# A macaron, convolution and latent-attention decoder layer on one core: the opening stage rebuilt, with products of ones ahead of the rows, sums of squares taken from rows, and the first two column tiles among the transposes

## The chip, the cores and the metric

One core of a Trainium2 chip runs the whole layer. The metric is the device time in microseconds. Three runs of the kernel before gave 1726.42, 1723.62 and 1724.4 us; their median is 1724.4 us.

## What is computed

One layer on 576 tokens (512 of a prompt, 64 new ones of eight sequences), 1024 channels, float32:

```
x = x + 1/2 * SwiGLU_FFN1(rmsnorm(x))
P = rmsnorm(x) @ w_in -> [GLU input | q_a | c_kv | k_pe | gate_a | gate_b]
A = conv branch (GLU, causal depthwise conv 31, LayerNorm, swish, projection)
B = latent attention with rotary keys, causal softmax, paged cache for the new tokens
x = x + w_out( sigmoid(gate_a) * A + sigmoid(gate_b) * B )
x = x + 1/2 * SwiGLU_FFN2(rmsnorm(x))
rmsnorm(x) = x * rsqrt(mean(x*x) + 1e-6) * g
swiglu_ffn(x) = (silu(h @ w_g) * (h @ w_u)) @ w_down,  h = rmsnorm(x), inner width 2816
```

The change touches only the start: the first rmsnorm and the first four of the 44 weight chunks of the first up-projection.

## The kernel before

**Layout.** The residual stream is kept transposed in SBUF: `xT` holds eight column tiles of 128 channels by 576 tokens (`KD` = 8, `T` = 576, `HALF` = 288). Every large product is made in three passes of fp32r: `x_hi` and `w_hi` are the rounded values, `x_lo` and `w_lo` what is left of them, and `product` (line 366) adds `w_hi*x_hi`, `w_hi*x_lo` and `w_lo*x_hi`, each over two halves of 288 tokens. So one column tile k of one weight chunk is 6 matmuls, and one chunk (8 tiles, 128 output channels) is 48. The row scale of rmsnorm (`rstd`) is applied to the outputs, not to x; so the products can start before it is known, but the first hidden tile can't be read out.

**Weights.** Chunk n (0, 1: gate and value columns of hidden tile 0; 2, 3: of tile 1; and so on) goes through a ring of 4 raw buffers and 2 hi buffers. SyncE's queue loads it in two DMAs (`load_chunk`, line 337); ScalarE copies it to `w_hibuf` (`split_hi`, 350), which from the third chunk on waits until chunk n-2 has been used up; GpSimd subtracts in four pieces (`split_lo`, 357), and TensorE waits for `w_lo_done` (`chunk`, 986).

**Opening.** SyncE issues the 5 DMAs of x rows (lines 462, 463) and then the 8 DMAs of chunks 0 to 3. ScalarE's queue issues 13 DMAs of gains, convolution weights and tables (661 to 670). TensorE waits for all 13 constants (`const_in`, 968), transposes the gains and the convolution weights, and then the x rows, 5 transposes for each column tile (973 to 984). VectorE copies each tile from PSUM to `xT` (1391, 1392), and one tile later makes `x_lo` (1371) and adds the squares into `sumsq` (1375, 1378). ScalarE makes square and `x_hi` of each tile (678, 679), with the hi copies of chunks 0 and 1 between tiles 0 and 2 (line 696). Only after all the transposes does TensorE begin chunk 0, tile by tile as `x_lo` comes (`x_ready`, 1004); `sums` (996) adds the squares over the partitions with a matrix of ones ahead of chunk 1; VectorE inverts (`inverse`, 1380), ScalarE takes the root (`rstd_root`, 681).

**Order that is written out by hand.** Each engine runs its own list in order. ScalarE's is `second_pair_hi` (708: hi of chunk 2, the root, hi of chunk 3), then `hidden(0)` (685: Silu, then `a_hi`), and only then the loop's `up_hi`, whose first item is the hi copy of chunk 4. VectorE's `hidden` (1402) scales the two products by `rstd` (1400), multiplies (1412) and makes `a_lo` (1414). TensorE needs the first PSUM unit read out, and the lo pieces of chunk 4, before it can start chunk 4.

Of the kernel before, what the change touches and what calls it, by code (L numbers as in the profile page):

```python
# [14 lines left out]
F32 = mybir.dt.float32  # L15
# [15 lines left out]
NT = PT_TILES + 1  # L31
DFF = 2816
# [21 lines left out]
KN, SQ = HH * DN, HH * DS_  # L54
KQ = KN + SQ
# [25 lines left out]
def layer(nc, x_prompt, x_sample, cache_ckv, cache_kpe, state_conv, page_table, w, const, out):  # L81

    ctx = ExitStack()
    with ctx:
# [50 lines left out]
        x_nat = place("x_nat", [P, NT, D], F32, A0 + 2 * XB)  # L135
        gain_rows = place("gain_rows", [NG, P], F32, A0 + 2 * XB + 4 * NT * D)
        conv_rows = place("conv_rows", [W, C], F32, A0 + 2 * XB + 4 * NT * D + 4 * P)
# [102 lines left out]
        stat = ps[:, 5:8, HALF:HALF + T // 3]  # L240


        const_in = sem("const_in")
# [191 lines left out]
        def _(sp):  # L435
# [25 lines left out]
            for i in range(PT_TILES):  # L461
                sp.dma_start(x_nat[:, i, :], x_prompt[0, i * P:(i + 1) * P, :]).then_inc(x_in, 16)
            sp.dma_start(x_nat[0:TS, PT_TILES, :], x_sample.rearrange("s t d -> (s t) d")).then_inc(x_in, 16)
            load_up(wv, n_ffn1_up, 0, 0, wait=False)
            load_up(wv, n_ffn1_up, 1, 1, wait=False)
# [103 lines left out]
        def _(pool):  # L569
            pool.memset(ones[:, :], 1.0).then_inc(ones_done, 1)  # L570

# [4 lines left out]
            with pool.Fori(0, FT // 2) as i:  # L576
                lo4(i * 4 + n_ffn1_up, n_ffn1_up, KD * P)
# [81 lines left out]
        def _(act):  # L659

            for name, row, k in (("norm_ffn1", G_FFN1, KD), ("norm_mix", G_MIX, KD), ("norm_ffn2", G_FFN2, KD),
                                 ("conv_b", G_CB, CT), ("conv_ln_g", G_LG, CT), ("conv_ln_b", G_LB, CT),
                                 ("q_a_norm", G_QA, QL // P)):
                act.dma_start(gain_rows[row:row + k, :], w[name][0].rearrange("(k p) -> k p", p=P)).then_inc(const_in, 16)
            act.dma_start(conv_rows[:, :], w["conv_w"][0]).then_inc(const_in, 16)
            act.dma_start(ident[:, :], const["ident"]).then_inc(const_in, 16)
            act.dma_start(causal[:, :], const["causal"]).then_inc(const_in, 16)
            act.dma_start(rope[:, :, :, :], const["rope"]).then_inc(const_in, 16)
            act.dma_start(kvg[:, :], w["kv_a_norm"][0:1, :].broadcast_to([P, KL])).then_inc(const_in, 16)
            act.dma_start(gqk[:, :], w["q_head_norm"][0:1, :].broadcast_to([P, DH])).then_inc(const_in, 16)  # L670

            def x_parts(v, t, c, gain, x_hi=x_hi):

                act.wait_ge(x_done, t + (KD * v + 1))
                if v or not isinstance(t, int) or t >= 2:
                    act.wait_ge(acc_done, t + (KD * v - 1))
# [4 lines left out]
            def rstd_root(v):  # L681
                act.wait_ge(inv_done, v + 1)
# [92 lines left out]
            act.wait_ge(acc_done, 2 * KD)  # L775
# [190 lines left out]
        def _(pe):  # L966

            pe.wait_ge(const_in, 13 * 16)
            pe.transpose(ps[:, 7, 0:NG], gain_rows[:, :], ident[0:NG, 0:NG])
            for c in range(CT):  # L970
                tr = pe.transpose(ps[:, 7, NG + c * W:NG + (c + 1) * W], conv_rows[:, c * P:(c + 1) * P], ident[0:W, 0:W])
            tr.then_inc(tr_done, 1)
            pe.wait_ge(x_in, 80)
            for t in range(KD):
                if t == 3:
                    pe.wait_ge(unit_read, 4)
                if t >= 4:
                    pe.wait_ge(x_done, t - 3)
# [967 lines left out]
```

## Time and profile before

| | before |
|---|---|
| median of 3 runs | 1724.4 us |
| the profiled execution's own time | 1725.19 us |
| its span | 1723.4 us |
| TensorE busy | 1633.0 us, 95% |
| VectorE, ScalarE, GpSimd busy | 744.2, 529.6, 603.8 us |
| HBM read | 117.79 MB |

A profile is one execution. The span is counted from its first instruction, and windows are microseconds from there. A matmul's duration holds the time that it spends in the pipe, so how fast matmuls go is read from start to start. The column PEclk is the granted TensorE clock as a share of 2.4 GHz; the clock's first record lies at about 36 us, and the profile prints 1.00 for everything ahead of it.

### The profile page before, as it was taken

What the parts mean: (1) busy time and instruction counts of PE and PEld (TensorE: products, weight loads), DVE (VectorE), ACT (ScalarE), POOL (GpSimd) and SP (SyncE); (2) the same over time, 40 slices, a digit from 0 to 9 for tenths busy, and PEclk for the clock granted to TensorE, in tenths of its full rate; (3) what the DMA queues carried; (4) which work ended last, traced back from release to release, by engine and by line L of the source; (5) the groups of instructions that cost most, each with busy time, mean ns of one, the idle gap of its engine ahead of it and who ended that gap; (6) DMA issues with size and microseconds to landing.
All of it is one profiled execution on the core that took longest, in us unless ns stands there. A gap on an engine that the chain in (4) does not pass through costs nothing.

```text
span 1723.4 us, 31031 instructions
## 1 busy us (share of the span) xinstructions
PE 1633.0 (95%) x11549; PEld 1545.2 (90%) x11549; DVE 744.2 (43%) x1148; ACT 529.6 (31%) x920; POOL 603.8 (35%) x693
## 2 busy tenths in 40 slices
PE   5999999999899999787999999999999999999998
PEld 4999999999899988365988888887999999999997
DVE  5322222212169866754566666664643222221001
ACT  3222222222221232242444444552333222222110
POOL 2455455444345545100000000001565455554441
PEclk9999999999999999897899999999999999999999
DMA  4222223222233322001212221212222222223221
GB/s 121 80 85 83 75 85 90 87 83 84 62 85 89 108 70 63 0 1 50 50 45 55 56 55 53 56 29 62 74 86 86 74 84 85 82 76 102 85 84 55
DMA packets 230066, 122.13 MB, mean 71 GB/s; under 512 B 28223, under 2 KB 226983, under 8 KB 229972
## 3 DMA queue, kind: packets, MB, share of 16 engines
q1 hardware_dynamic: 229150, 120.56, 24.3%
q8 instruction: 47, 0.77, 0.2%
q10 hardware_dynamic: 830, 0.48, 0.1%
q14 instruction: 39, 0.32, 0.1%
HBM read 117.79 MB, written 3.58 MB: 70 GB/s over the span
## 4 chain that ended last, share of the span: by engine, by line
PE 81%; DVE 8%; issue 4%; ACT 3%; POOL 2%; SPq 1%; DMA 1%; ACTq 0%; DVEq 0%; POOLq 0%
PE ps L376 61%; PE ps L1283 9%; PE ps L1226 3%; POOL w_lobuf L362 2%; PE ps L1133 1%; PE ps L1106 1%; PE ps L1212 1%; ACT prob L822 1%; DVE y L1455 1%; DVE page_ss L1848 1%; PE ps L1113 1%; PE ps L1252 1%; DMA gqk<-in_q_head_norm 1%; DVE s_buf L1740 1%; SPq L521 1%
## 5 line engine op out<-in xcount | busy, mean ns | idle before, releaser
L362 POOL TENSOR_TENSOR w_lobuf<-w_rawbuf,w_hibuf 128x256 fp32r<-128x256 f32 (+1 forms) x664 | 579.2, 903 | 651.8 <-ACT w_hibuf L355 651.8
L376 PE MATMUL ps<-x_hi,w_hibuf 128*128 128x288 f32 x1888 | 409.3, 298 | 6.8 <-POOL w_lobuf L362 3.1
L376 PE MATMUL ps<-x_lo,w_hibuf 128*128 128x288 f32 x1888 | 407.8, 298 | 0.0
L376 PE MATMUL ps<-x_hi,w_lobuf 128*128 128x288 f32 x1888 | 407.6, 297 | 0.0
L355 ACT ACTIVATE w_hibuf<-w_rawbuf 128x1024 fp32r<-128x1024 f32 (+1 forms) x166 | 185.2, 1115 | 667.7 <-PE ps L376 667.7
L376 PEld LDWEIGHTS ps<-x_hi,w_hibuf 128*128 128x128 f32 x1888 | 305.6, 189 | 9.0 <-issue 4.5
L376 PEld LDWEIGHTS ps<-x_lo,w_hibuf 128*128 128x128 f32 x1888 | 305.8, 189 | 0.4
L376 PEld LDWEIGHTS ps<-x_hi,w_lobuf 128*128 128x128 f32 x1888 | 305.6, 189 | 0.4
L376 PE MATMUL ps<-a_hi,w_lobuf 128*128 128x288 f32 x704 | 151.1, 296 | 0.0
L376 PE MATMUL ps<-a_hi,w_hibuf 128*128 128x288 f32 x704 | 151.0, 296 | 0.0
L376 PE MATMUL ps<-a_lo,w_hibuf 128*128 128x288 f32 x704 | 151.0, 296 | 0.0
L1400 DVE TENSOR_TENSOR tb<-ps,rstd 128x576 f32<-128x576 f32 x48 | 36.3, 757 | 248.2 <-PE ps L376 248.2
L1283 PE MATMUL ps<-kq_hi,cT_hi 128*128 128x288 f32 x512 | 125.4, 326 | 7.2 <-DVE cT_lo L1718 7.2
L1848 DVE TENSOR_REDUCE page_ss<-sq 128x8 f32<-128x512 f32 x128 | 85.0, 680 | 95.1 <-ACT sq L897 94.7
L1429 DVE SCALAR_TENSOR_TENSOR xT<-ps,xT 128x576 f32<-128x576 f32 x24 | 18.2, 758 | 247.7 <-PE ps L376 247.7
L644 POOL TENSOR_TENSOR ta<-kpe_nat 128x512 f32<-128x512 f32 x8 | 8.6, 1070 | 315.7 <-DMA kpe_nat<-in_cache_kpe 315.7
L376 PEld LDWEIGHTS ps<-a_hi,w_lobuf 128*128 128x128 f32 x704 | 113.7, 188 | 0.0
L376 PEld LDWEIGHTS ps<-a_hi,w_hibuf 128*128 128x128 f32 x704 | 113.7, 188 | 0.0
L376 PEld LDWEIGHTS ps<-a_lo,w_hibuf 128*128 128x128 f32 x704 | 113.7, 188 | 0.0
L1283 PE MATMUL ps<-kq_hi,cT_lo 128*128 128x288 f32 x512 | 110.4, 297 | 0.0
L1283 PE MATMUL ps<-kq_lo,cT_hi 128*128 128x288 f32 x512 | 110.3, 297 | 0.0
L1455 DVE SCALAR_TENSOR_TENSOR y<-ext,cols,y 128x512 f32<-128x512 f32 x120 | 104.5, 871 | 2.5
(266 smaller groups left out, 1992.0 us busy)
## 6 DMA issues: line engine op xcount, KB each, us to landing
w_rawbuf<-in_ffn_w_gu SPq DMA_DIRECT2D x176, 256.0 KB, 3.1
c_nat<-in_cache_ckv SPq DMA_DIRECT2D x128, 128.0 KB, 2.1
w_rawbuf<-in_w_in SPq DMA_DIRECT2D x58, 256.0 KB, 3.1
w_rawbuf<-in_ffn_w_down SPq DMA_DIRECT2D x32, 384.0 KB, 3.7
w_rawbuf<-in_ffn_w_down SPq DMA_DIRECT2D x32, 320.0 KB, 3.0
w_rawbuf<-in_w_out SPq DMA_DIRECT2D x16, 256.0 KB, 3.0
x_nat<-in_x_prompt SPq DMA_DIRECT2D x4, 512.0 KB, 4.9
w_rawbuf<-in_w_conv_out SPq DMA_DIRECT2D x8, 256.0 KB, 3.3
```

The lines of the kernel that those rows point to most:

```text
L355: act.activation(w_hibuf[:, r % HIS, 0:size], w_rawbuf[:, r, 0:size], ACT.Copy).then_inc(w_hi_done, 1)
L362: ins = pool.tensor_tensor(w_lobuf[:, r, part], w_rawbuf[:, r, part], w_hibuf[:, r % HIS, part].bitcast(F32), ALU.subtract)
L376: mm = pe.matmul(ps[0:width, 2 * s + h, 0:HALF], a, b[:, k, h * HALF:(h + 1) * HALF], start=first and i == 0 and j == 0, stop=last and i = ...
L521: page = sp.value_load(pages[0:1, ds(s * NP + t, 1)], min_val=0, max_val=cache_ckv.shape[1] - 1)
L822: act.activation(prob[:, qi, 0:(qi + 1) * P], ps[:, 2 + qi, 0:(qi + 1) * P], ACT.Exp, bias=small[:, 1, qi:qi + 1], scale=SCALE, accum_out= ...
L1106: mm = pe.matmul(ps[0:n, 2 * s + b, 0:QL], qaT[k][:, i * P:i * P + n], w_uq[:, k, b * QL:(b + 1) * QL], start=k == 0, stop=k == QL // P - 1)
L1226: mm = pe.matmul(ps[0:HQ, 7, 0:KL], s_buf[:, b, t, :], c_nat[:, b, t, :], start=t == 0, stop=False)
L1283: mm = pe.matmul(ps[:, page_banks(t) + half, 0:KQ], a, m[:, half, cols], start=k == 0 and j == 0, stop=k == 1 and j == 2)
L1400: return dve.tensor_tensor(halves(dst), unit(s)[0:rows], halves(rstd[0:rows, :]), ALU.mult)
L1429: dve.scalar_tensor_tensor(x2, unit(s), scale, x2, op0=ALU.mult, op1=ALU.add).then_inc(x_done, 1)
L1455: dve.scalar_tensor_tensor(dst, src, cw, dst, op0=ALU.mult, op1=ALU.add).then_inc(conv_p_step, 1)
L1848: dve.tensor_reduce(page_ss[:, t, :], sq[:, u, 0:H * DN].rearrange("p (h d) -> p h d", d=DN), AX, ALU.add).then_inc(page_red, 1)
```

## The change

It makes these edits.

1. The x rows are cut into six groups (128, 128, 32, 128, 128, 32 tokens) that don't cross the middle of the 576, and loaded by 7 DMAs. SyncE issues chunk 0 after them, waits for all x rows, issues chunk 1, waits for chunk 0, and issues chunks 2 and 3.
2. ScalarE's queue issues the identity and the first gain ahead of the other gains and the convolution weights; causal mask, rotary table, `kvg` and `gqk` are issued later, by `late_constants`, after the root in `second_pair_hi`. TensorE waits for two constants at the start instead of 13.
3. TensorE runs 30 products of a 128x128 matrix of ones with itself first.
4. Transposes of a tile use two PSUM units in turn. VectorE copies a tile with one instruction and makes its `x_lo` from PSUM right after ScalarE's `x_hi` of the same tile. TensorE puts the transposes of tile k+2 behind the product of chunk 0 with tile k, and then chunk 1 with tile k-4.
5. The squares are summed by ScalarE from the six row groups (with an accumulator); VectorE and ScalarE make the inverse root of a 128x6 tile; VectorE spreads it over six diagonal tiles; after chunk 2, TensorE transposes the other constants and multiplies the diagonals by ones (8 products), and VectorE copies the result to `rstd`.
6. The lo parts of chunks 0 and 1 are signalled piece by piece.

```diff
+X_GROUPS = ((0, 128), (128, 128), (256, 32), (288, 128), (416, 128), (544, 32))
+WARM = 30
@@ sync
+            for g, (t0, n) in enumerate(X_GROUPS):
+                prompt = max(0, min(n, TP - t0))
+                if prompt:
+                    sp.dma_start(x_nat[0:prompt, g, :], x_prompt[0, t0:t0 + prompt, :]).then_inc(x_in, 16)
+                if prompt < n:
+                    sp.dma_start(x_nat[prompt:n, g, :], new[t0 + prompt - TP:t0 + n - TP, :]).then_inc(x_in, 16)
+            load_chunk(sp, 0, 0, wv, 0, KD, 0, P, wait=False)
+            sp.wait_ge(x_in, 7 * 16)
+            load_chunk(sp, 1, 1, wv, 0, KD, DFF, P, wait=False)
+            sp.wait_ge(w_in_sem[0], 32)
+            load_chunk(sp, 2, 2, wv, 0, KD, P, P, wait=False)
+            load_chunk(sp, 3, 3, wv, 0, KD, P + DFF, P, wait=False)
@@ gpsimd
+            pool.memset(x_ss[:, :], 1.0).then_inc(ones_done, 1)
+            for n in range(2):
+                pool.wait_ge(w_hi_done, n + 1)
+                for c in range(4):
+                    part = slice(c * KD * P // 4, (c + 1) * KD * P // 4)
+                    pool.tensor_tensor(w_lobuf[:, n, part], w_rawbuf[:, n, part], w_hibuf[:, n, part].bitcast(F32), ALU.subtract)\
+                        .then_inc(w_piece, 1)
+                pool.wait_ge(w_piece, 4 * n + 4)
+                pool.sem_inc(w_lo_done, 1)
@@ scalar
+            act.dma_start(ident[:, :], const["ident"]).then_inc(rows_in, 16)
...
+            def row_squares(g):
+                n = X_GROUPS[g][1]
+                act.activation(x_sq[0:n, :], x_nat[0:n, g, :], ACT.Square, accum_out=x_ss[0:n, g:g + 1]).then_inc(x_squared, 1)
+                act.wait_ge(x_squared, g + 1)
+            act.wait_ge(x_in, 7 * 16)
+            act.wait_ge(ones_done, 2)
             act.wait_ge(unit_read, 4)
             for t in range(KD):
-                x_parts(0, t, t, G_FFN1)
                 if t < 2:
                     split_hi(act, t, t, KD * P, free=False)
+                act.wait_ge(x_done, t + 1)
+                act.activation(x_hi[:, t, :], xT[:, t, :], ACT.Copy, scale=cols[:, G_FFN1 + t:G_FFN1 + t + 1]).then_inc(xh_done, 1)
+                if t % 2 and t < KD - 1:
+                    row_squares(t // 2)
+            row_squares(3)
@@ second_pair_hi
                 split_hi(act, n0 + 2, (n0 + 2) % RAWS, KD * P)
-                rstd_root(v)
+                if v:
+                    rstd_root(v)
+                else:
+                    row_squares(4)
+                    row_squares(5)
                 split_hi(act, n0 + 3, (n0 + 3) % RAWS, KD * P)
+                if not v:
+                    act.wait_ge(x_inv, 1)
+                    act.activation(x_ss[:, :], x_ss[:, :], ACT.Sqrt).then_inc(x_root, 1)
+                    late_constants()
@@ tensor
+            pe.wait_ge(ones_done, 1)
+            for _ in range(WARM):
+                pe.matmul(ps[:, 0, 0:P], ones[:, :], ones[:, :], start=True, stop=True)
+            pe.wait_ge(rows_in, 2 * 16)
+            pe.transpose(ps[:, 3, 0:KD], gain_rows[0:KD, :], ident[0:KD, 0:KD]).then_inc(tr_done, 1)
+            pe.wait_ge(x_in, 7 * 16)
+            def x_transposes(t):
+                if t >= 2:
+                    pe.wait_ge(xl_done, t - 1)
+                for g, (t0, n) in enumerate(X_GROUPS):
+                    tr = pe.transpose(ps[:, 4 + 2 * (t % 2) + t0 // HALF, t0 % HALF:t0 % HALF + n],
+                                      x_nat[0:n, g, t * P:(t + 1) * P], ident[0:n, 0:n])
                 tr.then_inc(tr_done, 1)
+            def first_pair():
+                LAG = 4
+                x_transposes(0)
+                x_transposes(1)
+                pe.wait_ge(unit_read, 4)
+                for k in range(KD):
+                    first_chunk(0, k)
+                    if k + 2 < KD:
+                        x_transposes(k + 2)
+                    if k >= LAG:
+                        first_chunk(1, k - LAG)
+                for k in range(KD - LAG, KD):
+                    first_chunk(1, k)
+            def first_rstd():
+                pe.wait_ge(const_in, 7 * 16)
...
+                pe.wait_ge(x_spread, 1)
...
+                            mm = pe.matmul(stat0[:, b, a - b * third:z - b * third], ones[0:n, :], x_diag[0:n, g, a - t0:z - t0],
+                                           start=True, stop=True)
+                mm.then_inc(x_rstd, 1)
@@ ffn, the first one
+                    first_pair()
+                    chunk(2, 2, q_up + 2, (q_up + 2) % 4, range(KD), x_hi, x_lo)
+                    first_rstd()
+                    chunk(3, 3, q_up + 3, (q_up + 3) % 4, range(KD), x_hi, x_lo)
+                    up_pair(n_up, q_up, 2, 0, **x)
+                    pe.wait_ge(tables_in, 4 * 16)
@@ vector
             for t in range(KD):
+                xs = ps[:, 4 + 2 * (t % 2):6 + 2 * (t % 2), 0:HALF]
                 dve.wait_ge(tr_done, t + 2)
+                dve.tensor_copy(halves(xT[:, t, :]), xs).then_inc(x_done, 1)
+                dve.wait_ge(xh_done, t + 1)
+                dve.scalar_tensor_tensor(halves(x_lo[:, t, :]), xs, cols[:, G_FFN1 + t:G_FFN1 + t + 1],
+                                         halves(x_hi[:, t, :]).bitcast(F32), op0=ALU.mult, op1=ALU.subtract).then_inc(xl_done, 1)
+            dve.wait_ge(x_squared, NX)
...
+            for g in range(NX):
+                n = X_GROUPS[g][1]
+                ins = dve.tensor_scalar(x_diag[0:n, g, 0:n], ident[0:n, 0:n], x_ss[0:n, g:g + 1], None, ALU.mult)
+            ins.then_inc(x_spread, 1)
+            dve.wait_ge(x_rstd, 1)
+            dve.tensor_copy(rstd[:, :].rearrange("p (b n) -> p b n", b=3), stat0)
+            dve.tensor_copy(cols[:, KD:NCOL], ps[:, 3, HALF + KD:HALF + NCOL]).then_inc(rstd_done, 1)
```

## Rows read from the trace of the kernel before

**Rows 1.** Busy time of each engine by stretch: window, length, busy (instructions), PEclk, DMA share, GB/s.
```profile
0.00:40.00 40.00, 20.91 (x92) 16.84 (x93) 20.05 (x34) 13.77 (x19) 8.06 (x13) 1.00 0.43 123
84.00:200.00 116.00, 116.00 (x873) 116.00 (x872) 29.00 (x36) 30.42 (x36) 60.19 (x72) 1.00 0.27 81
```

**Rows 2.** Chain that ended last, 0 to 80 us: start, us, what.
```profile
6.02 10.11 DMA gqk<-in_q_head_norm
...
41.34 38.67 PE ps L376 x290
```

**Rows 3.** Timeline 0 to 30 us: start, us, engine, line, operation, idle before.
```profile
0.72 0.20 POOL L570 MEMSET ones<- 128x128 f32 x1 [0.29 <-POOLq L1936]
...
4.96 0.54 ACTq L668 DMA_DIRECT2D rope<-in_rope  x1
...
18.03 1.01 PEld L982 LDWEIGHTS ps<-ident,x_nat 64*128 64x128 f32 x5 [0.33 <-issue]
...
19.37 1.01 PEld L982 LDWEIGHTS ps<-ident,x_nat 64*128 64x128 f32 x5 [0.33 <-issue]
...
19.41 1.28 ACT L678 ACT_TABLE_LOAD   x1 [19.41 <-DVE xT L1392]
```

**Rows 4.** Arrival of the x rows and weights: us from issue to landing, 0 to 45 us.
```profile
L463 SPq DMA_DIRECT2D x_nat<-in_x_sample x1: 644/644/644, 2.6 to 2.6; - x1
DMA to landing us min/median/max: 3.6/5.4/7.6
```

**Rows 5.** Busy time by stretch, 8 to 12 us (last column: GB/s).
```profile
8.00:12.00 4.00, 0.00 (x0) 0.00 (x0) 0.00 (x0) 0.00 (x0) 0.00 (x0) 1.00 1.13 257
```

**Rows 6.** VectorE's, ScalarE's instructions by line, duration ns min/median/max.
```profile
L1371 DVE SCALAR_TENSOR_TENSOR x_lo<-xT,cols,x_hi x8: 802/819/1233, 22.1 to 38.4; 128x576 fp32r<-128x576 f32 x8
L1400 DVE TENSOR_TENSOR ta<-ps,rstd x22: 758/758/758, 46.9 to 310.2; 128x576 f32<-128x576 f32 x22
L679 ACT ACTIVATE x_hi<-xT,cols x8: 757/760/762, 21.3 to 37.6; 128x576 fp32r<-128x576 f32 x8
L355 ACT ACTIVATE w_hibuf<-w_rawbuf x5: 1039/1057/1062, 22.0 to 54.2; 128x1024 fp32r<-128x1024 f32 x5
```

**Rows 7.** Timeline 30 to 70 us, chunks 0 and 1 and the first hidden tile.
```profile
30.46 0.82 PE L376 MATMUL ps<-x_hi,w_hibuf 128*128 128x288 f32 x2 [1.88 <-DVE xT L1392]
...
35.39 0.68 PE L376 MATMUL ps<-x_lo,w_hibuf 128*128 128x288 f32 x2
...
35.87 0.68 PE L376 MATMUL ps<-x_hi,w_lobuf 128*128 128x288 f32 x2
...
40.20 1.14 PE L1001 MATMUL ps<-sumsq,ones 128*128 128x192 f32 x6
...
41.60 2.82 POOL L362 TENSOR_TENSOR w_lobuf<-w_rawbuf,w_hibuf 128x256 fp32r<-128x256 f32 x4 [10.87 <-ACT w_hibuf L355]
...
48.91 1.28 ACT L688 ACT_TABLE_LOAD   x1
...
51.79 0.69 ACT L690 ACTIVATE a_hi<-tb 128x576 fp32r<-128x576 f32 x1 [0.90 <-DVE tb L1412]
...
54.18 1.06 ACT L355 ACTIVATE w_hibuf<-w_rawbuf 128x1024 fp32r<-128x1024 f32 x1 [1.70 <-PE ps L376]
```

**Rows 8.** Timeline near 60 us, TensorE at the end of chunk 3.
```profile
60.24 0.32 PEld L376 LDWEIGHTS ps<-x_hi,w_hibuf 128*128 128x128 f32 x2
```

**Rows 9.** Timeline 606 to 632 us, TensorE: transposes, a wait, products.
```profile
615.09 3.49 PE L1082 MATMUL ps<-ident,latT 128*128 128x128 f32 x24
621.43 1.46 PE L1082 MATMUL ps<-ident,latT 128*64 128x128 f32 x6 [2.85 <-DVE lat L1536]
622.82 0.85 PE L376 MATMUL ps<-x_hi,w_hibuf 128*128 128x288 f32 x2
...
627.18 0.43 PE L376 MATMUL ps<-x_hi,w_hibuf 128*128 128x288 f32 x2
```

**Rows 10.** Busy time by stretch: prompt attention, 778 to 781 us.
```profile
778.00:781.00 3.00, 2.51 (x22) 2.20 (x21) 2.65 (x7) 1.40 (x4) 0.00 (x0) 1.00 0.00 0
```

More of the change, by code:

```diff
@@ L31 @@
 NT = PT_TILES + 1
+X_GROUPS = ((0, 128), (128, 128), (256, 32), (288, 128), (416, 128), (544, 32))
+NX = len(X_GROUPS)
 DFF = 2816
@@ L458, in load_merge @@
                 sp.dma_start(dst[:, CT:KD, :], src[:, :, (t + 1) * P:(t + 2) * P]).then_inc(w_in_sem[n % RAWS], 16)
[L461 to L465, printed above, removed]
+            new = x_sample.rearrange("s t d -> (s t) d")
+            for g, (t0, n) in enumerate(X_GROUPS):
[10 more added lines that the diff above has]
+            load_chunk(sp, 3, 3, wv, 0, KD, P + DFF, P, wait=False)
             with sp.Fori(1, FT // 2) as i:
@@ L574, in lo4 @@
                     split_lo(pool, n + g, (n0 + g) % RAWS, size)
-            with pool.Fori(0, FT // 2) as i:
+            for n in range(2):
[6 more added lines that the diff above has]
+                pool.sem_inc(w_lo_done, 1)
+            for n in range(2, 4):
+                split_lo(pool, n, n, KD * P)
+            with pool.Fori(1, FT // 2) as i:
                 lo4(i * 4 + n_ffn1_up, n_ffn1_up, KD * P)
@@ L774, in _ @@
             act.wait_ge(filled, 2)
-            act.wait_ge(acc_done, 2 * KD)
+            act.wait_ge(acc_done, KD)
             for i in range(NT):
@@ L966, in _ @@
         def _(pe):
[L968 to L978, printed above, removed]
-                for i in range(NT):
-                    n = P if i < PT_TILES else TS
-                    c = (i % PT_TILES) * P
-                    tr = pe.transpose(ps[:, 2 * (t % 4) + i // PT_TILES, c:c + n],
-                                      x_nat[0:n, i, t * P:(t + 1) * P], ident[0:n, 0:n])
-                tr.then_inc(tr_done, 1)
+            pe.wait_ge(ones_done, 1)
@@ new lines, in first_chunk @@
+            def first_chunk(n, k):
+                pe.wait_ge(xl_done, k + 1)
+                pe.wait_ge(w_piece, 4 * n + k // 2 + 1)
+                mm = product(pe, n, n, range(k, k + 1), x_hi, x_lo, w0=k, first=k == 0, last=k == KD - 1)
+                if k == KD - 1:
+                    mm.then_inc(w_used, 1)
+            def first_pair():
[11 more added lines that the diff above has]
+                    first_chunk(1, k)
@@ new lines, in first_rstd @@
+            def first_rstd():
+                pe.wait_ge(const_in, 7 * 16)
+                pe.transpose(ps[:, 3, HALF:HALF + NG], gain_rows[:, :], ident[0:NG, 0:NG])
+                for c in range(CT):
+                    pe.transpose(ps[:, 3, HALF + NG + c * W:HALF + NG + (c + 1) * W], conv_rows[:, c * P:(c + 1) * P], ident[0:W, 0:W])
+                pe.wait_ge(x_spread, 1)
+                pe.wait_ge(ones_done, 1)
+                third = T // 3
+                for g, (t0, n) in enumerate(X_GROUPS):
+                    for b in range(3):
+                        a, z = max(t0, b * third), min(t0 + n, (b + 1) * third)
+                        if a < z:
+                            mm = pe.matmul(stat0[:, b, a - b * third:z - b * third], ones[0:n, :], x_diag[0:n, g, a - t0:z - t0],
+                                           start=True, stop=True)
+                mm.then_inc(x_rstd, 1)
@@ L1363, in _ @@
         def _(dve):
+            dve.memset(tb[:, :], 0.0).then_inc(al_done, 1)
             dve.wait_ge(tr_done, 1)
-            dve.tensor_copy(cols[:, :], ps[:, 7, 0:NCOL]).then_inc(unit_read, 4)
-            dve.memset(tb[:, :], 0.0).then_inc(al_done, 1)
+            dve.tensor_copy(cols[:, G_FFN1:G_FFN1 + KD], ps[:, 3, 0:KD]).then_inc(unit_read, 4)
             def x_low(v, t, c, gain, hi, lo):
```

68 lines of the change are left out of this document (38 added, 30 removed).

## The prediction

> **What bounds the kernel now.** I read the busy times by stretch first. From 84 to 200 us TensorE is busy in every microsecond and issues 873 matmuls in 116 us, 0.133 us each; in the first 40 us it is busy for 20.9 [rows 1]. So only the opening has slack to win, and what is won there moves all that follows, since TensorE is the chain from 41.34 us on [rows 2]. The end point of my sum is the first matmul of chunk 4: chunk 1 begins at about 41.0, and three chunks of 48 matmuls at 0.133 us (6.4 us) put chunk 4 at 60.24 [rows 2, 8].
>
> The chain shows what the opening is made of: TensorE waits until 16.1 us for the last constant, `gqk` [rows 2]; eight tiles of transposes at 1.34 us each follow (from 18.03 to 19.37) [rows 3]; products start at 30.46 and chunk 0 ends at 40.2, held by VectorE, which makes a copy, `x_lo` and a sum of squares of each tile [rows 7].
>
> **TensorE's clock.** The clock column has no record here, so I read the level from the pace. Pairs of products go every 0.48 us (35.39 to 35.87), 0.24 us for one of 288 columns, which is 1.2 GHz, and stay at this until about 36.2, 5.8 us after the products began [rows 7]; later one goes every 0.133 us, 2.4 GHz [rows 1]. The nine microseconds of transposes from 17 us on did not raise it. At 615 us 24 transposes and a wait of 2.85 us are followed by products at the low level (durations 0.85), and it is high again at 627.2, 4.4 us after they began [rows 9]. A mixed stretch in which TensorE is busy for 2.51 of 3 us keeps the high level [rows 10].
>
> **The change, part by part** (times from the start of the span).
>
> *Constants and rows.* The wait for `gqk` goes. What is late next is the x rows: the last landed 7.6 us after its issue at 2.6, so at 10.2 [rows 4]; with 4 small tables out of the way I take 9.8 (9.3 to 10.2). Chunk 0's 512 KB come behind them on the same queue; at 257 GB/s [rows 5] that is 2 us, so 12 us (11.5 to 13.2).
>
> *Products of ones.* They start at 0.97, when the ones are set (0.72+0.20) [rows 3]. The profile shows a float32 product as two matmuls: three products of 192 columns are 6 in 1.14 us, 0.163 apart [rows 7], so 0.108 for 128 columns at the high level, 0.133 if the weight load sets the pace, and 0.213 at the low one. Of 60, 27 pass in the 5.8 us that the clock took in rows 7; 33 more take 3.6 to 4.4: the end is at 10.4 to 11.2. Never raised, it is 60 x 0.213 = 12.8, so 13.8. I take 11.0. It hides the wait for the rows, and is 1.2 us longer.
>
> *To the first `x_lo`.* Gain transpose, copy to `cols`: unit_read at 11.6. ScalarE now waits for chunk 0 (12.0) ahead of its first instruction, then table load 1.28 [rows 3], hi copy 1.04, `x_hi` 0.76 [rows 6]: 15.2. `x_lo` has only one SBUF input now besides PSUM; the nearest row is the scaling from PSUM, 0.758 in all 22 [rows 6], not the 0.80 to 1.23 of L1371 beside GpSimd. With 0.1 for semaphores: 16.1. GpSimd's first piece (0.7) is in time.
>
> On the table load the row shows 1.28 us. The Trainium skill (ScalarE: Activation LUTs, What ACT_TABLE_LOAD costs) adds about 1.38 us of drain to each switch. At 48.91 the load ends at 50.19, and multiply and `a_hi` end by 52.48 [rows 7], which leaves no room for a drain; with the page's figure my sum would be some 2.8 us later (two loads on the path), without it it stands.
>
> *Tiles 1 to 7.* They are now serial between VectorE and ScalarE: copy 0.76, `x_hi` 0.76, `x_lo` 0.76, 0.1 of semaphores, 2.4 us a tile (2.3 to 2.6). ScalarE's hi copy of chunk 1 (1.06) and the squares of the row groups (about 1.3 by L355's 1.06 plus an accumulator read) lie in the time in which VectorE works on. If TensorE keeps up, `x_lo` of tile 7 is there at 16.1+7x2.4 = 32.9, and five parts of 0.8 us (tile 7 of chunk 0, tiles 4 to 7 of chunk 1) end the pair at 36.9; with TensorE's own excess at tiles 4 and 5 I say **37.5**.
>
> *Does it keep up?* Between 11 and 16.1 TensorE has only tiles 0 and 1 to transpose and waits some 2.5 us. That is the picture of rows 9, after which the clock was low. At the low level a product part takes 6x0.24 = 1.44, a tile's transposes 1.6 (1.34 [rows 3] and a second cut at 32 rows), so 3.05 us for tiles 0 to 3 and 4.5 where chunk 1 joins: more than VectorE's 2.4. Tile 4's turn begins at 16.1+4x3.05 = 28.3 and ends at 32.8; high from there, tile 5's takes 2.6, and eight parts of 0.8 are left: **41.8, I take 42**. High from 28.3 on gives 40; only at 37.3, 44; still low in the last parts, 45.
>
> The Trainium skill (TensorE: Matmul & The Clock Gate, What's actually happening) says that "the default state is throttled, and activity releases the throttle". By that rule alone the products of ones release it and the opening is fast, my first rival; rows 9 speak for the low level instead.
>
> *Chunk 2.* Its hi copy waits for the end of chunk 0, 4.0 us ahead of the pair's end; 1.06 for hi, 2.82 for lo [rows 7] and 0.2: a wait of 0.1 to 1.2. I take 0.5. Then 6.4.
>
> *Root on TensorE.* Today `sums` costs 1.1 ahead of chunk 1. Now 5 small transposes and 16 matmul instructions of 32 to 128 columns come after chunk 2: bounds 1.0 (as today's sums) and 3.1 (0.163 each and 0.5); I take 2.4, nearer to the weight loads' pace. ScalarE's root and VectorE's six diagonals are hidden under chunk 2 (6.4 us). The four late DMAs are at most 0.54 each on ScalarE's queue [rows 3], 2.2 us, under chunk 2 as well; uncovered they would cost that.
>
> *Chunk 3, then chunk 4.* Here a new wait appears. The hi copy of chunk 4 stands on ScalarE behind `hidden(0)`, which now can't start until the sums behind chunk 2. Today `a_hi` ends at 52.48, 1.70 ahead of the release of that copy at 54.18 [rows 7]. After: copy of `rstd` 0.76, rest of `cols` 0.3, scaling 0.76, table load to the end of `a_hi` 3.57 (48.91 to 52.48), hi 1.06, lo 2.82 to 3.9, semaphores 0.4: 9.7 to 10.8 us, against 6.4 of chunk 3. TensorE waits 3.3 to 4.4 us; I take 3.4. Chunks 5 and on have their slack back.
>
> *Sum* for the pair's end at 42: 0.5+6.4+2.4+6.4+3.4 = 19.1, so chunk 4 at 61.1 against 60.24: +0.9. The wait of 3.4 us can let the clock fall once more, which rows 9 price at some 2 us (4.4 us of products at half pace); at 3 in 10 that is +0.6. **+1.5 us.** The profiled execution's own time is 1725.19 (span 1723.4), so 1726.7 by it; it lay 0.8 above the median of the three runs, and I state the forecast against the median: 1724.4+1.5, rounded to **1726.0 us**. Its own range is 1724 to 1728. About 0.2%, 3.45 us, is what a measurement of this kernel tells from no change.
>
> **Rivals.**
> 1. *The clock stays high.* Pair's end 37.5, chunk 4 at 56.6: -3.6 us, 1720.8; with sums of 1.0 us, 1719.4. For it: the mixed stretch of rows 10. Against: that stretch has no wait of 2.5 us. Chance 0.20, over half of it beyond 0.2%.
> 2. *The low clock lasts until products stand alone* (slower). TensorE's turn at tiles 0 to 5 is the place, 3.05 and 4.5 us against 2.4. It decides if the level is still low at about 35 us: pair's end 44 to 45, chunk 4 at 63.1 to 64.1, +3 to +4, and +2 when the wait at chunk 4 drops the clock: some 1729.5. For it: transposes among the products, which alone never raised it. Against: TensorE has no gaps then. Chance 0.26, 0.22 beyond 0.2%.
> 3. *No wait at chunk 4*, because VectorE and ScalarE are through sooner than their order says: 3.4 and 0.6 less, 1722; with a high clock 1717. Against: the order is fixed. Chance 0.12, 0.08 beyond.
> 4. *The products of ones don't raise the clock.* They end at 13.8, all parts are low: pair's end 46 or later, 1730 or more. Against: products raised it in both rows. Chance 0.08.
>
> The forecast keeps 0.34, nearly all within 0.2%. So faster 0.12+0.08 = 0.20, slower 0.22+0.06 to 0.08 and a little of the forecast = 0.32, same 0.48. The range: 1719.5 leaves out the low end of rivals 1 and 3, 1730.5 that of rivals 2 and 4, some 0.2 together.
>
> **What would show it.** Right: ones ending near 11; first product near 16; pace 0.24 from there to about 33; the pair's end near 42; a wait of TensorE for `w_lobuf` of 3 to 4 us ahead of chunk 4. Wrong: pace 0.133 all through, sums under 1 us, or no wait at chunk 4. If VectorE's step is over 2.6 us a tile, my term for the serial chain is the fault.

## The result, and the profile after

| | before | after |
|---|---|---|
| median of 6 runs each | 1724.6 us | 1731.2 us (1730.5 to 1733.4) |
| the profiled execution's own time | 1725.19 us | 1731.6 us |
| its span | 1723.4 us | 1729.8 us |
| first product | 30.46 us | 19.29 us |
| end of chunks 0 and 1 | 47.5 us | 47.5 us |
| chunk 2, 3, 4 begin | 47.58, 53.98, 60.38 us | 47.82, 57.31, 65.59 us |

The ratio is 1.0039, 95% interval 1.0026 to 1.0052: 6.6 us slower, just above the forecast range (1719.5 to 1730.5) and 5.2 us above the forecast of 1726.0. The first matmul of chunk 4 starts at 60.38 us before (the row of [rows 8], 60.24, is the last weight load of chunk 3) and at 65.59 after, so the opening alone explains 5.2 us. Two runs of the experiments below, of 1818.1 and 2022.2 us at mean granted clocks of 0.84 and 0.74, fell into a slow state of the chip and are in no median.

Busy times by stretch of the kernel after, in the columns of [rows 1]:

```profile
2.00:10.00 8.00, 8.00 (x58) 7.88 (x57) 0.00 (x0) 0.00 (x0) 0.00 (x0) 1.00 1.00 299
12.00:16.00 4.00, 3.18 (x12) 1.69 (x12) 0.76 (x1) 0.68 (x1) 0.00 (x0) 0.53 0.57 161
16.00:20.00 4.00, 0.71 (x3) 0.74 (x4) 1.48 (x2) 3.38 (x5) 2.25 (x4) 0.50 0.84 237
28.00:39.00 11.00, 11.00 (x43) 8.78 (x42) 5.04 (x7) 3.87 (x7) 0.00 (x0) 0.50 0.00 0
39.00:40.00 1.00, 1.00 (x6) 0.56 (x4) 0.00 (x0) 0.00 (x0) 0.00 (x0) 0.71 0.00 0
40.00:47.00 7.00, 7.00 (x52) 6.82 (x52) 1.58 (x2) 4.98 (x8) 2.06 (x3) 1.00 0.25 73
```

Here the clock column has records, the first at 5.5 us. Until then the matmul instructions of the products of ones start every 0.213 us, from then on every 0.111 us: the level rose there. It fell at 12.3 us (0.53 over 12 to 16), when TensorE had waited 1.7 us for the x rows and had just begun their transposes; the longer wait for chunk 0, from 15.2 to 19.3, came after that. It stayed at 0.50, which is 1.2 GHz, through the steps of the tiles, and rose only at 39.6 (0.71 over 39 to 40). Between 28 and 39 TensorE is busy in every microsecond and still issues only 43 matmuls.

The chain of waits after, 4 to 66 us (start, us, what), shows what the engines waited for:

```profile
4.75 10.48 DMA w_rawbuf<-in_ffn_w_gu
...
15.32 1.28 ACT L368
16.61 1.06 ACT w_hibuf L368
17.67 0.67 ACT x_hi L741
18.34 0.02 issue
18.37 0.83 DVE x_lo L1497
19.20 0.09 issue
19.29 1.78 PE ps L389 x6
21.07 1.53 PE ps L1036 x6
22.59 1.74 PE ps L389 x6
24.33 1.53 PE ps L1036 x6
```

Chunk 0 lands at 15.2 us, and from there to 19.3 everything waits for the row of table load, hi copy, `x_hi` and `x_lo`. Then TensorE alone is the chain: a product part and the transposes of a tile, 3.27 us together. The timeline after (as in [rows 3, 7]) has the waits of the other engines:

```profile
11.92 3.26 PE L1036 MATMUL ps<-ident,x_nat 128*128 128x128 f32 x12 [1.70 <-DMA x_nat<-in_x_sample]
...
22.63 0.76 DVE L1495 COPY xT<-ps 128x576 f32<-128x576 f32 x1 [1.12 <-PE ps L1036]
...
54.97 2.42 PE L1077 MATMUL ps<-x_diag,ones 128*128 128x128 f32 x16
...
65.59 0.54 PE L389 MATMUL ps<-x_hi,w_hibuf 128*128 128x288 f32 x2 [1.62 <-POOL w_lobuf L375]
```

The copy of a tile waits for TensorE, not the other way round. The root stage goes from 54.3 to 57.31, and at chunk 4 TensorE waits for `w_lobuf`, whose hi copy stands behind the first hidden tile.

### The profile page after: what moved, and what is told of

Same layout as the page of the kernel before. It is cut to its first block, busy times and chain, and to the rows that moved or that the text cites. A ratio compares the mean times of both kernels' runs of the same rounds, so it can differ in the third digit from the quotient of the medians.

```text
span 1729.8 us, 31160 instructions
## 1 busy us (share of the span) xinstructions
PE 1649.6 (95%) x11628; PEld 1558.5 (90%) x11628; DVE 737.1 (43%) x1140; ACT 531.0 (31%) x924; POOL 601.3 (35%) x694
## 4 chain that ended last, share of the span: by engine, by line
PE 81%; DVE 7%; issue 4%; ACT 3%; POOL 2%; SPq 1%; DMA 1%; DVEq 0%; ACTq 0%; POOLq 0%
PE ps L389 61%; PE ps L1386 9%; PE ps L1329 3%; POOL w_lobuf L375 2%; PE ps L1236 1%; PE ps L1209 1%; PE ps L1315 1%; ACT prob L878 1%; DVE y L1569 1%; DVE page_ss L1962 1%; PE ps L1216 1%; DMA w_rawbuf<-in_ffn_w_gu 1%; PE ps L1355 1%; DVE s_buf L1854 1%; SPq L542 1%
## 5 line engine op out<-in xcount | busy, mean ns | idle before, releaser
L375 POOL TENSOR_TENSOR w_lobuf<-w_rawbuf,w_hibuf 128x256 fp32r<-128x256 f32 (+2 forms) x656 | 570.9, 901 | 643.9 <-ACT w_hibuf L368 643.9
```

What stands on the lines that cost most here:

```text
L375: ins = pool.tensor_tensor(w_lobuf[:, r, part], w_rawbuf[:, r, part], w_hibuf[:, r % HIS, part].bitcast(F32), ALU.subtract)
```

## The experiments

No kernel here leaves a part of the computation out; products of ones are extra work and their results are not used. Behind each expectation stand the median time and its ratio to the kernel before on the same chip (median 1724.7 to 1725.3 us), with the 95% interval. Moments inside a kernel are read from one profiled execution of it.

**The products of ones.** Left out:

```diff
-WARM = 30
+WARM = 0
```

> The changed kernel without the 30 products of ones. Clock theory: the level they raised was lost at 12.3 us, before the first product of weights at 19.3, so they buy nothing: within 1 us of the changed kernel, first product still near 19.3 and pace 0.24 us until about 39. Rival: they are worth the transposes' speed or bring the later rise forward; without them it is slower by 2 us or more.

1732.0 us, ratio 1.0034 (1.0020 to 1.0048). The first product came at 19.77 and the level rose at 44.6. The medians don't tell this version from the kernel after (1731.2, ratio 1.0039). In the profiled executions chunk 4 began 2.2 us later without the ones (67.83 against 65.59), since the level rose 5 us later, but the moment of the rise varies from run to run, as shown below. So no gain by the 30 products in front is shown: their high level is gone before the first product of weights. Held over the gap instead, with 8 more in front:

```diff
-WARM = 30
+WARM = 38
@@ first_pair, behind x_transposes(1)
+                for _ in range(20):
+                    pe.matmul(ps[:, 0, 0:P], ones[:, :], ones[:, :], start=True, stop=True)
```

> The changed kernel with 38 products of ones ahead of the rows and 20 more between the transposes of tile 1 and the first product of weights (TensorE idles there from 15.2 to 19.25). Clock theory: the level stays high, VectorE's 2.4 us a tile sets the step instead of TensorE's 3.27, and the pair ends near 41 instead of 47.5: 6 us faster than the changed kernel, about 1725. Rival (rows, weights and the serial chain are the cost, not the clock): less than 1.5 us faster, or slower by the 20 products if they run late.

1724.2 us (9 runs), ratio 1.0004 (0.9991 to 1.0016): by the ratio nearly all of the 6.6 us of the change are gone, though the first product came only 0.3 us earlier (19.03). Two of the nine runs took 1730.9, with a mean granted clock of 0.976 against 0.981 in the other seven. Busy times by stretch of this kernel, beside those above:

```profile
16.00:20.00 4.00, 3.65 (x31) 3.48 (x31) 1.48 (x2) 3.39 (x5) 2.51 (x4) 1.00 0.89 257
28.00:39.00 11.00, 10.61 (x74) 9.62 (x74) 4.88 (x7) 6.53 (x11) 1.02 (x2) 1.00 0.07 18
```

The same 11 us take 74 matmuls instead of 43, at 1.00 instead of 0.50 (from 33.15 us on they are products alone, since this kernel is further on). Chunk 2 began at 40.87 instead of 47.82. The clock over the opening is worth what the change lost. The 38 in front without the 20 in the gap were not run, so this run doesn't say which of the two groups did it.

**The table load.** A one-column Square at the start loads the table early:

```diff
+            act.activation(sq[:, 0, 0:1], ones[:, 0:1], ACT.Square)
             act.wait_ge(x_in, 7 * 16)
```

> The changed kernel with one small activation on ScalarE at the start, so that the table load lies in the wait for the rows. Chain theory: the first product comes 1.3 us earlier (18.0) and all after it, 1730.0. Rival: the step of 3.27 us is fixed by TensorE but its start moves too, so it gives the same 1.3; if it gives nothing, the start of the chain is elsewhere (arrival of chunk 0's weights at 15.3).

1730.5 us, 1.0027 (1.0016 to 1.0038). First product 1.5 us earlier (17.79), but the level rose at 42.4 instead of 39.6, and chunk 2 began at 48.0 against 47.8. While the pair runs at the low level, a start brought forward is given back if the rise comes later. That the early table made it come later is not shown: the version with ScalarE's order changed (below) has the program of the kernel after up to chunk 2, and in its profiled execution the level rose at 44.4 instead of 39.6. Over the seven profiled executions whose tiles all ran at the low level, the rise came either 18.7 to 20.3 us behind the first product, in or right behind the first twelve matmuls that follow each other without transposes (after, and two versions below), or 24.6 to 24.8 us behind it, in the last 24 (here, without the ones, and two versions below).

**The constants alone**, on the kernel before: identity first, the four tables late.

```diff
+            act.dma_start(ident[:, :], const["ident"]).then_inc(const_in, 16)
...
-            pe.wait_ge(const_in, 13 * 16)
+            pe.wait_ge(const_in, 9 * 16)
```

> The kernel before, with one part of the change alone: identity first on ScalarE's queue, the four tables issued after the root, TensorE waits for 9 constants instead of 13. Part theory: the wait for gqk until 16.1 us was the only thing ahead of the transposes, the x rows were there at 10.2; all that follows moves by 5 to 6 us, 1719 us. Rival: the weights of chunk 0 (landed by 13.2) or VectorE's steps take up the gain: less than 2 us faster.

1723.3 us, 0.9989 (0.9980 to 0.9999). Waits of this kernel, 0 to 40 us (us in total, times, longest):

```profile
PE ps L973 <- DMA conv_rows<-in_conv_w: 13.8, 1, 13.8
```

A wait until 16.1 became one until 13.8, and that is the 2 us. With the DMA of `conv_rows` moved to second place:

> e1_tables with one more move: the convolution weights' DMA right behind the identity's. In e1_tables TensorE still waited for them until 13.83 us, with the x rows there at about 10.3. If the queue's order is the reason, TensorE starts at 10.5 to 11.5 and the time falls by 2 to 3 us below e1_tables, about 1720.5. Rival: ScalarE's hi copies then wait for chunk 0's weights (13.2), and only 1 us is gained.

1722.9 us, 0.9987 (0.9977 to 0.9996); TensorE waited until 13.76, now for `gain_rows`. So the order on the queue is not what holds them. With 44 products of ones in that wait:

> e1_tables (order of the kernel before) with 44 products of ones while TensorE waits for the constants. Theory: in the old order VectorE's three operations per tile (2.1 to 3.1 us) set the pace, and TensorE at the high level only ends chunk 0 sooner by the few tenths it is behind: 0 to 1 us faster than e1_tables. Rival: the low level costs the old order too, half of the 5.7 us of products at half pace, 2 to 3 us.

1722.9 us, 0.9986 (0.9977 to 0.9996). The level was high from 6.6 to 23.7 and low again when the products began at 27.48. It is the result of the run without them.

**x rows on another queue**: the three DMAs of 32 rows on ScalarE's.

```diff
+                if row == G_FFN1:
+                    act.dma_start(x_nat[0:32, 2, :], x_prompt[0, 256:288, :]).then_inc(x_in, 16)
...
```

> The changed kernel with the three 32-row DMAs of x on ScalarE's queue instead of SyncE's. In the changed kernel the first transpose of x waits until 11.92 us, against rows complete at 10.2 before. If the small DMAs hold up the queue, the rows are complete by about 10.5 and chunk 0's weights by 14; if the DMA engines' total work is the limit, within 0.3 us of 11.9. The time itself stays within 1 us of the changed kernel either way, since the clock's rise sets the pair's end.

One run, 1733.3 us. Its timeline:

```profile
2.62 0.74 ACTq L699 DMA_DIRECT2D x_nat<-in_x_sample  x1
...
11.84 2.31 PE L1038 MATMUL ps<-ident,x_nat 128*128 128x128 f32 x12 [0.89 <-DMA x_nat<-in_x_sample]
```

The last DMA of rows was issued at 2.6 us, as in the kernel before, and the first transpose of x still waited for it until 11.84 (11.92 after); chunk 0 landed at 15.9. So the moment of issue is not what makes the rows late.

**ScalarE's order at chunk 4**: its hi copy ahead of the first hidden tile, the loop's first pass written out.

```diff
+                    split_hi(act, n0 + 4, n0 % RAWS, KD * P)
+                    hidden(f, q0, 0, a_hi)
+                    split_hi(act, n0 + 5, (n0 + 1) % RAWS, KD * P)
+                    hidden(f, q0, 1, a_hi)
```

> The changed kernel with ScalarE's list put in another order: the hi copy of chunk 4 ahead of the first hidden tile, that of chunk 5 ahead of the second. If the 1.9 us that TensorE idles before chunk 4 come only from this order, they go, and all behind moves by 1.9: about 1.6 to 1.9 us faster than the changed kernel. Rival: the lo copy or the PSUM unit (read out from 58.7 on) is just as late, and nothing changes.

1728.2 us, 1.0015 (1.0005 to 1.0025), 3.0 us less than after. The wait is gone: chunk 3 began at 59.37 and chunk 4 6.5 us later, at 65.87, where the kernel after took 8.3 us. So the order is worth 1.8 us; the rest of the 3.0 is not explained. In this profiled run, the slowest of ten, chunk 3 was itself late, since the level rose at 44.4.

**All of these together**: g1's order, the early table, `WARM` 36, and in the gap 5 products of ones, the transposes of the constants and 9 more products.

> The changed kernel with the clock kept high (36 products of ones ahead, 14 more in the gap), the table loaded at the start, the transposes of the other constants in the gap too, and the order of g1. Sum: pair's end 40.9 as in e3_fill, less 1.4 for the table; 0.6 less behind chunk 2; no wait at chunk 4: chunk 4 at about 54.7 against 60.4 before, 5.5 us faster than the kernel before, 1719.5. Rival: the fill runs late (14 products and the constants outlast the hi copy, or conv_rows lands after 14 us) and eats 1 to 2 us of it; or the clock falls after all, then 1725.

1720.4 us (1718.9 to 1722.4), 0.9972 (0.9962 to 0.9981). The clock stayed high, first product 17.72, chunk 4 at 54.8. This kernel is the base of the next two. Without its first 36 products:

> g2_best without the 36 products of ones ahead of the rows; the 14 in the gap stay. Clock theory: transposes and 14 products from 11.4 on start at the low level, don't raise it before the first product, and TensorE's step stays at 3.27 us: the pair ends at 46 to 49, 6 to 8 us slower than g2_best, near 1727. Rival: the products in the gap alone are enough, within 1 us of g2_best.

1727.0 us, 1.0006 (0.9996 to 1.0016), in two clusters: 1724 to 1726 and 1728 to 1729. The level rose at 23.0, fell at 29.8 and rose at 40.1. So the products in the gap alone are not enough, as the 30 in front alone were not. With VectorE's copy of tile t+1 ahead of `x_lo` of tile t:

> g2_best with VectorE copying tile t+1 before it makes x_lo of tile t, so that ScalarE's x_hi no longer lies in VectorE's step. With the clock high the step of 2.35 us is VectorE's serial chain; it becomes copy plus x_lo, 1.6 us, and TensorE (0.8 + 1.1, and 2.7 where chunk 1 joins) sets the pace: the pair's end moves from 39.5 to about 37, 2.3 us faster than g2_best, 1718. Rival: ScalarE's squares of the rows, or the weights of chunk 1 (17.0), hold it: under 1 us.

1731.9 us, 1.0040 (1.0026 to 1.0054): my expectation fell. Waits of this kernel, 16 to 45 us:

```profile
DVE xT L1511 <- PE ps L1045: 18.2, 6, 3.4
PEld ps L389 <- DVE x_lo L1518: 7.8, 6, 1.7
```

TensorE issues the transposes of tile t+1 behind the product of tile t-1, and VectorE now held `x_lo` of tile t back for them. The loop of both waits made the first step 3.5 us (17.93 to 21.47); at 22.8 the clock fell, and from then on a step took 4.9 us.

**What holds chunk 0's weights.** Their arrival is the term of the forecast that failed: 12.0 forecast, 15.2 measured. SyncE issues chunk 1 only when chunk 0 has landed, on the kernel after, and on the best version with 9 fewer products in the gap:

```diff
             load_chunk(sp, 0, 0, wv, 0, KD, 0, P, wait=False)
-            sp.wait_ge(x_in, 7 * 16)
-            load_chunk(sp, 1, 1, wv, 0, KD, DFF, P, wait=False)
             sp.wait_ge(w_in_sem[0], 32)
+            load_chunk(sp, 1, 1, wv, 0, KD, DFF, P, wait=False)
```

> Edit: the changed kernel, with SyncE issuing chunk 1 only when chunk 0 has landed (after the change it is issued once the x rows have landed, at 11.9 us, and chunk 0 lands at 15.2 although the DMA engines move only 20 to 40 GB/s from 12.4 to 12.9 us). Theory A (chunk 0's last pieces are held up by chunk 1 on the same queue): chunk 0 lands at 12.9 to 13.5 instead of 15.2, the table load begins there, but chunk 1 then lands 1 to 2 us later than today, about 16.5 to 17, and its hi copy stands on ScalarE ahead of the x_hi of tile 1, so the first product comes at 17.0 to 17.5 and the second no sooner than 21; the clock is low in both, and the time stays within 2 us of 1731.2. Theory B (chunk 0 is late by itself): it lands at 15.2 or later, chunk 1 at 18 or later, and the kernel is 1 to 3 us slower than the changed one.

> Edit: the best version so far (table loaded early, products of ones in the gap, chunk 4's hi copy first), with chunk 1 issued only when chunk 0 has landed, its hi copy on ScalarE moved from ahead of tile 1's x_hi to ahead of tile 2's, and the second group of nine products of ones left out. Theory A (chunk 1 holds up chunk 0's last pieces): chunk 0 lands at about 13, first product at 15.6 to 16.0 (17.7 in the best version), clock high all through, chunk 4 at about 53 (54.8), 1718 to 1719.5 us against 1720.4. Theory B (chunk 0 is late by itself): it lands at 15 as before, first product at 17.7 to 18, and without the nine products the clock falls near 20 us, so chunk 4 comes at 60 or later and the time is 1725 or more.

1730.8 us, 1.0034 (1.0023 to 1.0046), and 1725.7 us, 1.0001 (0.9993 to 1.0010). Chunk 0 landed at 15.4 and 14.9, with nothing behind it: theory A fell. In the second, the shorter filling also cost the level in eleven of twelve runs (clocks 0.974 to 0.977; the twelfth, 0.982, took 1719.4). The first one shows what does hold it. DMA of this kernel, 12.6 to 13.0 us:

```profile
DMA packets 8, 0.01 MB, mean 24 GB/s; under 512 B 1, under 2 KB 4, under 8 KB 8
## 3 DMA queue, kind: packets, MB, share of 16 engines
q10 hardware_dynamic: 4, 0.01, 5.5%
q1 hardware_dynamic: 4, 0.00, 1.5%
```

Shares of 5.5% and 1.5% of sixteen engines are one engine and a little (0.88 and 0.24). Its packets alternate: one of the constants' queue (q10), one of the weights' (q1). The packets of 2 KB on q10 are the 31 rows of `conv_rows`. Read one by one from the trace, each starts when the one before has ended, from 9.4 us to 14.0: they are all on one DMA engine, and chunk 0's share of that engine goes between them. So `conv_rows` issued late (behind chunk 2's hi copy), on the kernel after and on the best version, and `conv_rows` split on the kernel with the constants alone:

```diff
-            act.dma_start(conv_rows[:, :], w["conv_w"][0]).then_inc(const_in, 16)
+            act.dma_start(conv_rows[0:16, :], w["conv_w"][0, 0:16, :]).then_inc(const_in, 16)
+            act.dma_start(conv_rows[16:W, :], w["conv_w"][0, 16:W, :]).then_inc(const_in, 16)
```

> Edit: the changed kernel, with the DMA of the convolution weights (31 rows of 2 KB) issued on ScalarE's queue behind the hi copy of chunk 2 instead of at the start. In the trace of the run with chunk 1 issued later, these 31 packets run one after the other on a single DMA engine until about 14.0 us, and 512-byte packets of chunk 0 alternate with them after all the other engines have gone idle at 12.4. Theory C (that one DMA engine holds up chunk 0): chunk 0 lands at 12.6 to 13.3 instead of 15.2, the first product comes at 16.5 to 17.2 (19.3), the rise of the clock is up to 2.5 us earlier, and the time is 1728.5 to 1731, since the clock is still low. Theory D (the convolution weights are a bystander): chunk 0 lands at 15 or later, the time is 1730.5 to 1732.

> Edit: the best version so far with the same late DMA of the convolution weights; the transposes of the constants go back behind chunk 2, and 7 products of ones fill the wait for chunk 0 instead of 14 and the transposes. Theory C: chunk 0 lands at 12.6 to 13.3, first product at 15.6 to 16.3 (17.7), clock high all through, the pair's end 1.5 to 2 us earlier, 1.0 us more for the root stage, which has the transposes again: chunk 4 at 53.5 to 54.5 (54.8), 1718.5 to 1720.5 us. Theory D: chunk 0 lands at 15, the first product waits 2 us behind the 7 products of ones and the clock falls: 1724 us or more.

> Edit: the version of the kernel before with the identity first and the four tables late, its convolution weights loaded in two DMAs, of 16 rows and of 15 rows. Theory C (all 31 rows go to one DMA engine, and TensorE waits for that engine until 13.8 us): if 16 rows are spread over the 16 DMA engines and only the other 15 share one, the constants are there at 12.0 to 12.8, the first product comes 1.0 to 1.8 us earlier than 28.1, and the time is 1721.5 to 1722.8 against 1723.3. If both halves go to one engine, or under theory D, TensorE waits until 13.5 to 14.2 and the time stays at 1723.

Late, after: 1729.1 us, 1.0024 (1.0012 to 1.0035); chunk 0 landed at 13.3 instead of 15.2:

```profile
13.36 1.28 ACT L368 ACT_TABLE_LOAD   x1 [13.36 <-DMA w_rawbuf<-in_ffn_w_gu]
```

The first product came at 17.32, the level rose at 36.7, and chunk 4 began at 63.25, 2.3 us earlier than after. Split: 1719.7 us, 0.9973 (0.9963 to 0.9982), about 3 us less than the version without the split (0.9989) and more than either theory gave, since the packets of the second part, of 15 rows, overlap too. Timelines of the first transposes, of that version and of the split one:

```profile
13.83 0.32 PE L973 MATMUL ps<-ident,gain_rows 39*128 39x39 f32 x1 [13.83 <-DMA conv_rows<-in_conv_w]
```

```profile
10.79 0.32 PE L974 MATMUL ps<-ident,gain_rows 39*128 39x39 f32 x1 [10.79 <-DMA conv_rows<-in_conv_w]
...
25.07 0.82 PE L376 MATMUL ps<-x_hi,w_hibuf 128*128 128x288 f32 x2 [1.88 <-DVE xT L1399]
```

The constants are there 3.0 us sooner, the products begin 3.0 us sooner (28.11 to 25.07), and the 2 KB packets now overlap, all within 7.7 to 9.5 us. Theory C stands. The kernel before has this hold-up too: its 31 packets run from 8.5 to 12.9 us. The late version of the best kernel took 1723.5 us, 0.9983 (0.9973 to 0.9992), in two clusters: five runs at 1718.0 to 1719.5 (0.981 to 0.982) and seven at 1723.3 to 1725.4 (0.976 to 0.979). To see whether TensorE's short waits in a tile's step let the clock fall, I built the best version with the split, 32 products in front and 2 instead of 9 behind the constants, and a twin with one product of ones more in each of the first four steps:

```diff
                         x_transposes(k + 2)
+                    if k < LAG:
+                        pe.matmul(ps[:, 2, 0:P], ones[:, :], ones[:, :], start=True, stop=True)
```

> Edit: the version with the table early, the gap filled and chunk 4's hi copy first, its convolution weights loaded in two DMAs of 16 and 15 rows, still at the start; 32 products of ones ahead of the rows, and in the gap 5 products, the transposes of the constants and 2 more products. Expected by theory C: constants there by 11.5, chunk 0 at 12.5 to 13.3, first product at 15.6 to 16.2 (17.7), no transposes of constants behind chunk 2, chunk 4 at 52.5 to 53.5 (54.8): 1718 to 1719 us if the clock stays high in every run. TensorE has some 0.35 us of waits in each tile's step, so the clock may fall in some runs, which would then take 1723 to 1725, as in the version with the late convolution weights.

> Edit: the same, with one more product of ones behind the transposes in each of the first four tiles' steps, where TensorE has some 0.35 us of waits (two matmul instructions, 0.27 us). If the falls of the clock come from these waits, every run keeps the high clock: 1718 to 1719.5 us, with a spread under 4 us, and fewer runs at 1723 to 1725 than its twin. If the products lie on the path instead, it is up to 1 us slower than the twin's runs with a high clock.

Without: 1718.3 us (1717.0 to 1726.9, 12 runs), 0.9964 (0.9954 to 0.9974), one run at 1726.9 with 0.974. With: 1717.4 us (1716.7 to 1718.5, 5 runs), 0.9956 (0.9943 to 0.9968), 7.6 us less than before and the best of the study. Busy times by stretch, of the one without and of the one with:

```profile
20.00:28.00 8.00, 6.70 (x41) 5.20 (x41) 5.41 (x8) 4.39 (x7) 0.22 (x1) 1.00 0.00 0
```

```profile
20.00:28.00 8.00, 8.00 (x49) 6.25 (x49) 5.41 (x8) 4.41 (x7) 0.11 (x1) 1.00 0.00 0
```

TensorE has no idle time left there, and VectorE does the same work: the extra products cost nothing. That they keep the level is not shown: one fall in 12 runs against none in 5 decides nothing.

## Why the prediction was wrong

The forecast was +1.5 us, and by its chances no change that can be told was the likeliest (0.48, slower 0.32); measured were +6.6 us, 0.7 us outside the range. The step that failed is the arrival of chunk 0's weights, 12 us forecast and 15.2 measured. The mechanism was that of the forecast's main line: the level is lost before the first product, and TensorE at the low level, not VectorE, sets the step. How long the low level lasted was rival 2's mechanism. Step by step:

1. **Arrival of rows and weights, the step that failed.** "With 4 small tables out of the way I take 9.8" and "so 12 us". Measured: rows 11.92, chunk 0 15.2. For the weights I divided bytes by the rate of all engines [rows 5]; they are there only when the slowest engine has its part, and that one had `conv_rows` to carry. The late DMA of `conv_rows` gave 1.9 us back (13.3). The other 1.3 us came with the rows: the last of their 4 KB packets ended at 11.1 us, 9.4 in the kernel before and 9.2 in the version with the constants alone, which keeps its 5 DMAs of rows. The new cut into six groups goes with the delay, but not through the later issue of the last DMA (3.8 instead of 2.6): issued at 2.6, the rows were there at 11.84. Why the rows are slower stays open.
2. **Products of ones.** End 11.0 forecast, 10.06 measured: they raised the clock in 4.5 us, not 5.8; rival 4 fell. The fall of the level was forecast for the wait behind the transposes; it came at 12.3, right behind the wait for the rows (12.8 to 15.1 in the five other profiled executions with products of ones in front and none in the gap), and in all of them ahead of the first product.
3. **To the first `x_lo`.** 4.1 us from landing forecast (12.0 to 16.1), 4.0 measured (15.2 to 19.2): right. So 3.1 us of the miss come from step 1 alone. The table load took 1.28 us and the hi copy starts as it ends (16.61). The Trainium skill (ScalarE: Activation LUTs, What ACT_TABLE_LOAD costs) adds some 1.38 us of drain; this trace has no room for it, so the row of the trace was the right price.
4. **Tile step at the low level.** 3.05 forecast, 3.27 measured: the transposes took 1.53 and the product part 1.74 with the change between them. From the first `x_lo` to the end of tile 4's turn that makes 17.8 us instead of 16.7, 1.1 more.
5. **The rise.** Forecast for the end of tile 4's turn, 32.8; shifted by the 4.2 us above that is 37.0, and it came at 39.6. At half pace this cost 1.2 us in tile 5's turn (3.8 instead of 2.6). This is rival 2's mechanism, the low level lasting until products stand nearly alone; I priced it with my own arrival (pair's end 44 to 45), not with a late one. The rise is also luck in part: in other executions it came up to 4.5 us later behind the first product. The last eight parts took 6.7 instead of 6.4. Pair's end: 41.8+3.1+1.1+1.2+0.3 = 47.5, as measured.
6. **From there to chunk 4.** Wait for chunk 2: 0.5 forecast, 0.3 measured. Chunks 2 and 3: 6.4 each forecast, 6.5 measured. Root on TensorE: 2.4 forecast, 3.0 measured, close to the upper bound. Wait at chunk 4: 3.4 forecast, 1.8 measured, since Silu's table load ran at 50.88, ahead of the wait that I had put it behind. The sum was 19.1, measured 18.1. No clock fall followed that wait.

So chunk 4 comes to 47.5+18.1 = 65.6, as measured, 5.2 us late. The remaining 1.2 us to the end are not settled: matched by instruction, the shift is 5.3 us until 373 us, 5.9 at 516 and 6.4 from 868 on, and my only reading is that later low stretches fall on other instructions. From chunk 4 to the end the profiled executions of all versions took 1661.8 to 1664.2 us (before 1663.0, after 1664.2), so 1.2 us is within what this stretch varies by.

What the change gained is real: products began 11.2 us earlier. But chunks 0 and 1 then took 28.2 us instead of 17.1, so their end did not move. With the level held over the gap they took 21.5; so some 6.7 us went into half the pace and 4.4 into the new order at the high level. Behind them, TensorE took 18.1 us to chunk 4 instead of 12.8, most of it the root (3.0) and the wait for chunk 4's `w_lobuf` (1.8): these are the 5.2 us.

## What to carry to other kernels

A head start on TensorE is worth only what its clock makes of it: price each step at both levels, and look at when the level rises, because that moment, more than the first product, sets the end of the stage. Work put in to raise the clock has to reach up to the first real product and fill the short waits behind it; 30 products that ended 9 us early bought nothing that the medians show; 8 more of them and 20 in the gap bought back nearly all of the 6.6 us. And look for small DMAs whose rows go out one after the other: one DMA of 31 rows held up a load of 512 KB by 2 us and the constants by 3, and two lines that split it gave about 3 us. Together with the tables issued late, on the old opening, that was as much (0.9973) as the rebuilt opening at its best had given until then (0.9972).

## What the runs showed that I had not expected

- The 31 rows of `conv_rows` (2 KB each, 84 to 165 ns a packet) went through one DMA engine in a row for 4.6 us; as 16 and 15 rows they overlapped and were through in 1.8 us. Why the DMA of 31 rows is not spread I can't say from these runs.
- On that engine packets of two queues alternate one for one, so a 512-byte packet of weights waited for a 2 KB packet of constants each time, while fifteen engines were idle.
- A product stage that is busy in every microsecond can stay at 1.2 GHz for over 20 us when small transposes stand between the products: low from 12.3 to 39.6 after, to 44.6 without the ones. Once high, such a mixture kept the level, with waits of 0.35 us a step, in most runs but not in all (by the mean clock in 11 of 12 runs with the split, in 5 of 12 with the late DMA on the best version).
- Some versions have two clusters of times 5 us apart (1718 to 1719.5 and 1723.3 to 1725.4), and the mean granted clock tells which run was which (0.981 and 0.976). It tells runs of one kernel apart, not kernels: the version without the ones has 0.981 at 1732.0 us, since its low stretch lies ahead of the clock's first record (44.6 us). A median of three runs of such a kernel can mislead by more than the effect under test.
